# The state-mixing layer of a four-layer encoder step, with its low-rank branches first and its key and decay work spread over the projections

## The reference

```
xx = h_prev - h;  xm[i] = h + xx * mu[i]          # six mixes: xr xw xk xv xa xg
r = xr @ w_rkv[0];  k = xk @ w_rkv[1];  v = xv @ w_rkv[2]
w_log = -softplus(-(w0 + tanh(xw @ w1) @ w2)) - 0.5;  decay = exp(-exp(w_log))
a = sigmoid(a0 + (xa @ a1) @ a2);  g = sigmoid(xg @ g1) @ g2
kk = k * k_k, divided by its norm over each head
k = k * (1 + (a - 1) * k_a)
S = S * decay + (S @ -kk) (kk * a)^T + v k^T;  y = S @ r   # per token
y = groupnorm(y) * ln_w + ln_b + sum(r * k * r_k) * v;  out = (y * g) @ w_out
```

## Time and profile before

| what | value |
|---|---|
| median of three runs | 1920.26 us |
| the profiled execution's own time | 1920.77 us |
| its span in the trace | 1918.8 us |
| PE busy | 1689.6 us, 88% of the span |
| weight load (PEld) busy | 1604.2 us, 84% |
| DVE busy | 1190.7 us, 62% |
| ACT busy | 841.1 us, 44% |
| POOL busy | 739.6 us, 39% |
| mean granted clock of TensorE | 0.941 |

### The profile page before, as it was taken

One profiled execution on the slowest core, in us unless ns is written; L12 is line 12 of the kernel. 1 busy time (PEld: TensorE's weight loads), 2 busy tenths in 40 slices (PEclk: granted clock), 3 DMA queues, 4 the chain that ended last, 5 costly groups with the idle time before them and its releaser, 6 DMA issues.

```text
span 1918.8 us, 37370 instructions
## 1 busy us (share of the span) xinstructions
PE 1689.6 (88%) x14101; PEld 1604.2 (84%) x14101; DVE 1190.7 (62%) x2041; ACT 841.1 (44%) x1561; POOL 739.6 (39%) x829
## 2 busy tenths in 40 slices
PE   4988999996776299799999968799999987999995
PEld 3867999995763299799999957699999975999994
DVE  3685777645526845567774446667774586677832
ACT  2444566432225033345653334456553345466532
POOL 5651566300011541036651116346641670366501
PEclk9998999997888599899999989899999988999997
DMA  6312555452320000345545511145544620455451
GB/s 154 115 46 86 141 146 152 136 154 85 110 66 6 0 3 10 95 124 145 149 135 149 157 41 49 57 132 153 153 130 141 169 83 23 135 150 153 127 150 59
DMA packets 342621, 204.95 MB, mean 107 GB/s; under 512 B 20898, under 2 KB 339640, under 8 KB 342384
## 3 DMA queue, kind: packets, MB, share of 16 engines
q1 hardware_dynamic: 338704, 196.27, 35.8%
q0 software_dynamic: 3808, 7.17, 1.4%
HBM read 199.92 MB, written 3.39 MB: 106 GB/s over the span
## 4 chain that ended last, share of the span: by engine, by line
PE 79%; DVE 10%; ACT 4%; POOL 3%; issue 3%; DMA 1%; ACTq 0%; DVEq 0%; POOLq 0%
PE bank L873 22%; PE bank L874 22%; PE bank L875 22%; PE bank L1149 4%; PE bank L884 2%; ACT LS L1471 1%; PE bank L1109 1%; DVE XX L2083 1%; ACT hi L1437 1%; DVE SW L1995 1%; DVE LS L1863 1%; DVE LS L1854 1%; DVE SC L1981 1%; POOL vrows L621 1%; DVE top L1992 1%
## 5 line engine op out<-in xcount | busy, mean ns | idle before, releaser
L873 PE MATMUL bank<-XH,hi 128*128 128x320 f32 (+2 forms) x2024 | 637.0, 315 | 32.9 <-issue 12.2
L1809 DVE TENSOR_TENSOR lo<-raw,hi 128x2048 fp32r<-128x2048 f32 (+4 forms) x201 | 425.7, 2118 | 360.6 <-ACT hi L1437 360.6
L874 PE MATMUL bank<-XL,hi 128*128 128x320 f32 (+2 forms) x2024 | 632.4, 312 | 0.0
L875 PE MATMUL bank<-XH,lo 128*128 128x320 f32 (+2 forms) x2024 | 632.1, 312 | 0.0
L873 PEld LDWEIGHTS bank<-XH,hi 128*128 128x128 f32 (+1 forms) x2024 | 382.9, 189 | 39.7 <-issue 26.4
L1437 ACT ACTIVATE hi<-raw 128x2048 fp32r<-128x2048 f32 (+3 forms) x205 | 359.6, 1755 | 72.4 <-PE bank L875 64.2
L874 PEld LDWEIGHTS bank<-XL,hi 128*128 128x128 f32 (+1 forms) x2024 | 383.2, 189 | 1.1
L875 PEld LDWEIGHTS bank<-XH,lo 128*128 128x128 f32 (+1 forms) x2024 | 382.8, 189 | 0.5
L685 POOL TENSOR_TENSOR upad<-upad,rstd 128x128 f32<-128x128 f32 (+1 forms) x176 | 168.6, 977 | 199.6 <-ACT upad L1517 199.6
L873 PE MATMUL bank<-GH,hi 128*128 128x322 f32 x704 | 219.2, 311 | 0.0
L874 PE MATMUL bank<-GL,hi 128*128 128x322 f32 x704 | 218.8, 311 | 0.0
(11 more groups left out here) (378 smaller groups left out, 2427.4 us busy)
## 6 DMA issues: line engine op xcount, KB each, us to landing
raw<-in_f_w_up SPq DMA_DIRECT2D x176, 512.0 KB, 5.0
raw<-in_f_w_down SPq DMA_DIRECT2D x64, 704.0 KB, 4.7
raw<-in_a_w_in SPq DMA_DIRECT2D x12, 1024.0 KB, 5.2
raw<-in_b_w_rkv SPq DMA_DIRECT2D x12, 1024.0 KB, 5.2
raw<-in_a_w_out SPq DMA_DIRECT2D x8, 1024.0 KB, 5.1
raw<-in_b_w_out SPq DMA_DIRECT2D x4, 1024.0 KB, 5.6
raw<-in_c_w_out SPq DMA_DIRECT2D x4, 1024.0 KB, 5.2
raw<-in_a_w_in SPq DMA_DIRECT2D x12, 256.0 KB, 4.2
```

What stands on the lines that cost most here:

```text
L873: pe.matmul(out, a, xh(k), start=(start and k == 0), stop=False)
L874: pe.matmul(out, a, xl(k), start=False, stop=False)
L875: last = pe.matmul(out, b, xh(k), start=False, stop=(stop and k == kt - 1))
L1809: dve.tensor_tensor(lo[n % 2][:, 0:w_], raw[n % 2][:, 0:w_], hi[n % 2][:, 0:w_].bitcast(F32), ALU.subtract).then_inc(w_lo, 1)
```

## The change

Only layer 1's mixer is touched. The order of the products becomes key, receptance, value. The low-rank weights move to where VV and G lie, and POOL loads them as soon as the layer before has made its last output tile; the three low-rank mixes are made first, into LW, A and K. Their first matmuls stand ahead of all products; the second ones go in groups of three between the first four products. The three large mixes are made tile by tile: DVE mixes into one of two small buffers (xn), ACT takes the high part, DVE the low part; the second mix has its own pair XH2, XL2. Products use two banks, not four. Decay, key norms and bonus are spread in the orders of all engines over products 12 to 23, tile by tile with two buffers each. Two exponentials replace three. POOL multiplies the keys, rates and receptance by the decays and the keys by their gain (four instructions a tile), and ACT scales the gate G behind the first chunk's evacuations. The cores of the edits:

```diff
# POOL
-                pool.wait_ge(mm_done, done_after[s0 + 11])
+                pool.wait_ge(x_done, 8 * xs_of[norm_of[layer, "mix"]] + 8)
...
+                for m in range(KD):
+                    pool.wait_ge(kk_used, m + 1)
+                    pool.tensor_tensor(A[:, m, :], A[:, m, :], XX[:, m, :], ALU.mult)
+                    pool.wait_ge(gain_done, m + 1)
+                    chain(pool.tensor_tensor(K[:, m, :], K[:, m, :], TK[:, m % 2, :], ALU.mult))
+                    pool.tensor_tensor(K[:, m, :], K[:, m, :], XX[:, m, :], ALU.mult)
+                    pool.wait_ge(rkv_evac, KD + m + 1)
+                    pool.tensor_tensor(R[:, m, :], R[:, m, :], HN[:, m, :], ALU.mult).then_inc(keys_done, 1)
...
+                pool.wait_ge(keys_done, KD)
+                pool.wait_ge(mm_done, done_after[s0 + 11])
                 side_by_side(0)
# PE
+                pe.wait_ge(lora_in, 96)
...
+                    for k in range(KD):
+                        pe.wait_ge(lora_mix, KD * a + k + 1)
+                        last = pe.matmul(psum[4 + a][r_, 0:T], L1[:, k, c_], (LW, A, K)[a][:, k, :], start=(k == 0), stop=(k == KD - 1))
...
+                def lora_rows(m):
+                    if m == 0:
+                        pe.wait_ge(shift_out, 1)
+                        pe.wait_ge(lora_act, 3)
+                    if m >= 2:
+                        pe.wait_ge(lora_evac, 3 * m - 3)
...
+                def key_sums(m):
+                    if m == 0:
+                        pe.wait_ge(lora_evac, 24)
+                    if m >= 2:
+                        pe.wait_ge(hs_root, m - 1)
+                    pe.wait_ge(kk_sq, m + 1)
+                    pe.matmul(psum[2 + m % 2][:, 0:T], C("headsum"), sq[:, m % 2, :], start=True, stop=True).then_inc(hs_done, 1)
+                def bonus_sums(m):
+                    if m >= 2:
+                        pe.wait_ge(bonus_out, m - 1)
+                    pe.wait_ge(bonus_in, m + 1)
...
+                sums_at = {13: (0, 1), 14: (2, 3), 15: (4, 5), 16: (6, 7)}
+                bonus_at = {19: (0,), 20: (1,), 21: (2, 3), 22: (4, 5), 23: (6, 7)}
+                for i in range(24):
+                    n, j = s0 + i // 2, i // 8
+                    ready(n)
+                    if i >= 2:
+                        pe.wait_ge(rkv_evac, i - 1)
+                    product(psum[i % 2][:, 0:T], n, 128 * (i % 2), lambda k: xh[:, k, :], lambda k: xl[:, k, :],
+                            before=(lambda k: pe.wait_ge(mix_done, KD * j + k + 1)) if i % 8 == 0 else None)
+                    if i < 4:
+                        lora_rows(2 * i)
+                        lora_rows(2 * i + 1)
# ACT
+                def high(j, k):
+                    act.wait_ge(mix_raw, KD * j + k + 1)
+                    act.copy((XH, XH2, XH)[j][:, k, :], xn[:, k % 2, :]).then_inc(mix_hi, 1)
+                def key_squares(m):
+                    if m >= 2:
+                        act.wait_ge(hs_done, m - 1)
+                    act.activation(sq[:, m % 2, :], K[:, m, :], ACT.Square, scale=vcol("b_k_k", m)).then_inc(kk_sq, 1)
+                def key_roots(m):
+                    act.wait_ge(hs_done, m + 1)
+                    if m >= 2:
+                        act.wait_ge(kk_used, m - 1)
+                    act.activation(xn[:, m % 2, :], psum[2 + m % 2][:, 0:T], ACT.Sqrt).then_inc(hs_root, 1)
+                def key_gain(m):
+                    if m >= 2:
+                        act.wait_ge(keys_done, m - 1)
+                    act.activation(TK[:, m % 2, :], A[:, m, :], ACT.Identity, scale=vcol("b_k_a", m), bias=onemka[:, m:m + 1]).then_inc(gain_done, 1)
+                middle(0)
+                high(0, 0)
+                middle(1)
+                highs(0, 1, 8)
+                middle(2)
+                for i in range(4):
+                    tile(i)
+                    if i % 2:
+                        split_hi(s0 + i // 2 + 2)
+                    lora_rows(2 * i)
+                    lora_rows(2 * i + 1)
+                highs(1, 0, 4)
+                tile(4)
+                highs(1, 4, 8)
+                tile(5)
+                split_hi(s0 + 4)
...
+                act.wait_ge(cc_done, KD)
+                chain(act.activation(XX[:, :, :], HN[:, :, :], ACT.Exp, scale=-DECAY))
+                act.activation(HN[:, :, :], HN[:, :, :], ACT.Exp, scale=DECAY).then_inc(decay_done, 1)
+                tile(12)
+                key_gain(0)
+                key_gain(1)
+                tile(13)
+                split_hi(s0 + 8)
+                for i in range(14, 18):
+                    m = 2 * (i - 14)
+                    key_roots(m)
+                    key_roots(m + 1)
+                    if m + 3 < KD:
+                        key_squares(m + 2)
+                        key_squares(m + 3)
+                    tile(i)
+                    if i % 2:
+                        split_hi(s0 + i // 2 + 2)
+                    if m + 3 < KD:
+                        key_gain(m + 2)
+                        key_gain(m + 3)
...
                 turned_parts(0)
+                act.wait_ge(bonus_out, KD)
+                for m in range(KD):
+                    ins = act.activation(G[:, m, :], G[:, m, :], ACT.Copy, scale=vcol("b_ln_w", m))
# DVE
+                mix(0, 0, 8)
+                split_lo(s0 + 1)
+                split_lo(s0 + 2)
+                dve.wait_ge(lora_out, 24)
+                mix(1, 0, 4)
+                split_lo(s0 + 3)
+                mix(1, 4, 8)
+                split_lo(s0 + 4)
+                dve.wait_ge(mm_done, done_after[s0 + 3])
+                mix(2, 0, 4)
+                split_lo(s0 + 5)
+                mix(2, 4, 8)
+                split_lo(s0 + 6)
...
+                def key_heads(m):
+                    dve.wait_ge(hs_root, m + 1)
+                    t = xn[:, m % 2, :]
+                    chain(dve.tensor_scalar(t, t, 1e-12, None, ALU.max))
+                    chain(dve.reciprocal(t, t))
+                    chain(dve.scalar_tensor_tensor(out=t, in0=K[:, m, :], scalar=vcol("b_k_k", m), in1=t, op0=ALU.mult, op1=ALU.mult))
+                    dve.scalar_tensor_tensor(out=chunks(MX[:, m, :], 1, 64), in0=chunks(t, 1, 64), scalar=-1.0,
+                                             in1=chunks(HN[:, m, :], 0, 63), op0=ALU.mult, op1=ALU.mult)
+                    dve.tensor_scalar(chunks(MX[:, m, :], 0, 1), chunks(t, 0, 1), -1.0, None, ALU.mult)
+                    dve.wait_ge(gain_done, m + 1)
+                    dve.tensor_tensor(A[:, m, :], t, A[:, m, :], ALU.mult).then_inc(kk_used, 1)
...
+                key_heads(0)
+                key_heads(1)
+                split_lo(s0 + 8)
+                key_heads(2)
+                key_heads(3)
+                split_lo(s0 + 9)
+                for m in range(4, 8):
+                    key_heads(m)
+                split_lo(s0 + 10)
+                dve.wait_ge(kk_used, KD)
+                bonus_rows(0)
+                bonus_rows(1)
+                split_lo(s0 + 11)
+                for m in range(KD):
+                    bonus(m)
+                    if m + 2 < KD:
+                        bonus_rows(m + 2)
```

More of the change, by code:

```diff
@@ L361, in build @@
         VV = take("VV", [128, KD, T])
-        LW = take("LW", [128, KD, T])
+        over_s = over + 7 * size([128, KD, T])
+        take = region(over_s + size([128, KD, T]))
         G = take("G", [128, KD, T])
@@ L1112, in pe_rwkv @@
[L1112 to L1116, removed]
-                                  start=True, stop=True).then_inc(lora_out, 1)
[L1119 to L1124, removed]
@@ L1664, in evac @@
+                for i in range(18, 24):
+                    tile(i)
+                    if i == 19:
+                        split_hi(s0 + 11)
                 def evac(name, c, dst):
@@ new lines, in mixed, with mix, low @@
+                def mixed(dst, k, mu):
+                    return dve.scalar_tensor_tensor(out=dst, in0=XX[:, k, :], scalar=vcol("b_mu", 8 * mu + k),
+                                                    in1=HN[:, k, :], op0=ALU.mult, op1=ALU.add)
+                for a, mu in enumerate((1, 4, 5)):
+                    for k in range(KD):
+                        mixed((LW, A, K)[a][:, k, :], k, mu).then_inc(lora_mix, 1)
+                def mix(j, first, end):
+                    lows = (XL, XL2, XL)[j]
+                    def low(k):
+                        dve.wait_ge(mix_hi, KD * j + k + 1)
+                        dve.tensor_tensor(lows[:, k, :], xn[:, k % 2, :], (XH, XH2, XH)[j][:, k, :].bitcast(F32), ALU.subtract
+                                          ).then_inc(mix_done, 1)
+                    for k in range(first, end):
+                        if KD * j + k >= 2:
+                            dve.wait_ge(mix_done, KD * j + k - 1)
+                        mixed(xn[:, k % 2, :], k, (2, 0, 3)[j]).then_inc(mix_raw, 1)
+                        if k > first:
+                            low(k - 1)
```

(13 more changed lines are left out.)

191 lines of the change are left out of this document (70 added, 121 removed).

## The result

The changed kernel takes 1868.26 us in the median of four runs (1866.00 to 1870.22), against 1920.22 (1919.88 to 1923.24) for the kernel before on the same chip: 0.9726 of its time, 95% interval 0.9708 to 0.9743, so 52 us less. The forecast was 1876 us, with 1863 to 1890 as its range.

A forecast was written before the change was run, and what follows sets the result against it. PE, busy 88% of the span, was taken to be shortenable only where it waits in layer 1's mixer. The walk moved the second stage from 678.15 to 633.5, gaining 44.6 us from 1920.77: 1876 us, range 1863 to 1890.

The forecast's parts named there:

- the walk: Prediction's step-by-step sum through layer 1's mixer, from weight loads to the first chunk's second stage at 633.5 us.
- Rival A: Key-head stretch: the round through DVE, POOL and ACT sets the pace, about 13 to 17 us each; 1876 us; chance 0.50.
- One sign: Timeline from about 539 to 595 us: PE should be mostly idle at the low clock.
- Rival D: Layer 1's mixer: products hide everything and PE is the bound; gain of 96 us, 1825 us; chance 0.05.
- E: POOL's 12 path instructions held up by DVE's two-input ones; at 6.4 us each 1942 us; slower, chance 0.03.
- F: No change: time comes back because the recurrence or output slab loads end at a fixed time; chance 0.02.
- Rival B: Key-head rounds without the lock's charges: 8.2 us less, 1864 to 1869 us; chance 0.19.
- the lock's charge: Key-head rounds, DVE and POOL blocking each other: 0.9 us a round, and 2.3 in the first two; 8.2 in sum.
- The step on the rounds: Four pairs of key-head tiles handed round DVE, POOL and ACT: 56.7 us in sum, ending at 595.3.
- the stalls: Products 4 to 11, waiting for evacuations with two banks: five small stalls of 0.8 to 1.1 us, 4.3 in sum.
- the slow restart of 3.0: PE after standing since product 19: 3.0 us extra around products 20 to 23.
- the scalings: Eight scalings of G on ACT ahead of the first square's evacuation: 8 x 0.55 = 4.4 us on the path.

The follow-up runs named there:

- the experiment: Changed kernel with DVE making the ninth slab's low part before the first key_heads, not behind the second: 1863.26 us in one run.
- two load semaphores: Changed kernel with the first low-rank matmuls waiting for the first three weight loads only, the second ones for the other three: 1865.41 us in one run.
- the four edits: Changed kernel with key gains behind the roots, gate scalings on POOL, ninth slab's low part first and two groups of weight loads: 1848.53 us.
- The last edit: Changed kernel with the four edits plus ACT's inverse square root in place of root and DVE reciprocal: 1841.17 us, 0.9595 of the kernel before.

## Why the prediction was right, and where its sum was off

Its steps against the changed kernel's trace, in us after the norm's reciprocal (those of the walk less 433.98):

| point | walk | trace |
|---|---|---|
| first low-rank matmul | 10.6 | 11.0 |
| third nonlinearity done | 30.9 | 30.0 |
| last of the second low-rank matmuls ends | 55.2 | 52.5 |
| product 11 out | 87.7 | 83.4 |
| exponentials done | 98.9 | 94.0 |
| first pair's clip | 104.6 | 99.4 |
| last `key_heads` done | 161.3 | 152.1 |
| bonus sums end | 185.7 | 176.3 |
| second stage of the first chunk | 199.5 | 188.4 |

So this stretch gave 244.2 - 188.4 = 55.8 us, where 44.6 were forecast. Two things took a part back: the 96 matmuls at the lower clock 2.4, and a layer that began 2.9 later in this execution. 55.8 - 2.4 - 2.9 = 50.5, and the profiled times differ by 50.55. So close an agreement is partly luck: what follows those 96 matmuls took from 1235.6 to 1237.6 us in the ten traces. It is luck too that the two took back half of what the walk had overstated: it missed the second stage by 11 us, and the profiled time missed the forecast by only 6 (8 in the median).

**The bound was named rightly.** Rival A, the round through three engines, is what the trace shows, by pair distances, by the key gain's wait for POOL, and by POOL's busy time (33.0 in 56 us, 28 forecast; the difference is stretched instructions). Moving the two key gains of each round gave 11.9 us. One sign held only in part: PE was to be idle mostly and at the low clock, and worked for 27 of 56 us at a granted clock of 0.77, between the two levels. Rival D, PE as the bound, is excluded by PE's 27 busy us of 56; E by POOL's instructions, the longest of which took 2.84 in the rounds and 2.92 behind them; F because the gain of the stretch arrived at the end of the kernel. Rival B is wrong in what it denies, though its time (1864 to 1869) holds the median: the lock's charge is there, one low part costing 2.0 us in the experiment. The time came out at B's end for other reasons.

**The mis-sized terms**, in order. The step on the rounds was too long: 16.5, 16.5, 14.2 and 9.5, together 56.7, measured 15.24, 15.26, 13.37 and 8.86, together 52.7. `key_heads` took 4.0 and, beside POOL, 4.7, not 4.3 and 5.2; the charge for the low part was 2.3 and measured 2.0. The second low-rank matmuls were priced at 3 x 0.57 = 1.71 a group and took 1.475: two of the three run together, though each step is then 0.74 long and not 0.57. That is 1.9 us over eight groups. The first-stage ones took 15.2 instead of 16.5; the records of two branches overlap there too (454.06 starts within the line above it). Of products 4 to 11, the stalls were 4.3 by the walk and 2.7 measured (83.4 - 52.5 = 30.9 us, where eight at 3.52 are 28.2). From product 11 to the first clip it took 16.0 where the walk has 16.9. At the end the slow restart of 3.0 was close (2.5), the scalings cost 3.7, not 4.4, and they began 0.9 earlier, because ACT's evacuations ahead of them ran beside PE's work and not after it. Every one of these errors is under 3 us but the rounds, and nearly all have the same sign; that is why they made 11 us. In `key_heads` the steps of the reciprocal (2.19) and of the product behind it (0.58) came out as priced; the error lies in the clip (0.36, not 0.48) and in the instructions that don't wait for one another, whose records overlap (0.48 for two, not 0.59; 0.40, not 0.47).

**Slips in the prediction's own working**: the third nonlinearity, from 463.5 with 1.28 and 0.43, ends at 465.2, not 464.9. The POOL instruction of 6.39 us is a scaling by a vector, and others of its kind took 1.08, not the 0.86 of the product it is compared with. The range begins at 1863, 1 below B's lower end. None of this moves the forecast by more than 1 us.

**Not seen at all**: that the pause of the scalings would put the stage behind it on the lower clock (2.4 us), and that DVE's mixes follow the loads so closely that the two nearly tie.

**The second buffers** did what the walk says: the gaps of 5.75 are gone, and taking the overlap away from one change of mix cost 6.8. What the other parts of the change gave one by one (the early weight loads, the interleaved low-rank matmuls, the tile-by-tile key work) no run separates.

The Trainium skill (TensorEngine Tiling (Array Packing), section "Overview") holds that a contraction over 64 rows or fewer leaves TensorE underused, and that splitting it into independent tiles can be up to twice as fast there. Here two such matmuls of different branches, whose operands lie in different halves of the partitions, took 0.74 us together, as long as the single one over 128 rows behind them, with nothing set for it in the code. Against twice 0.57 that is about 1.5 times as fast; with the slower third one it bears on this kernel by 1.9 us.

What stays open: the restart took from 20.15 to 21.03 us in the changed kernel and in all its edits but the last. In the changed kernel full-speed records (0.31 us) come back 5.0 us after it begins, with two load semaphores 3.3. The length of the idle time ahead of it does not order these (1.87 us with the four edits, 20.17; 6.17 with two load semaphores, 20.15; 7.69 in the changed kernel, 20.85). What decides this was not tried, and it makes single differences under 1 us of this stretch unsafe to read. The last edit differs plainly: PE was at full-speed records already and stood for only 0.77 us, and the stretch took 18.65.

## What to carry to other kernels

When work is spread over three engines in a ring, look at every queue for an instruction that waits for the previous turn and stands ahead of the next one's first: moving such a pair in each of three turns gave 12 us here without removing any work. Put a long DVE instruction with two SBUF inputs where POOL rests, not beside it. Price a pause of PE by its restart as well, and before speeding up what releases a wait, ask what would release it next and how far behind that is.

## What the runs showed of the hardware that was not expected

- Under short alternating instructions both sides of DVE and POOL lose: 0.86 became 0.94 to 1.20 on POOL and about 0.5 became 1.04 on DVE, and a DVE clip with one SBUF input went from 0.32 to as much as 1.00. The one long instruction cost POOL 2.0 us at a time.
- A pause of PE of 4.26 us made the following 96 small matmuls take 5.39 us instead of 3.02; with a pause of 0.73 they took 3.02. In the traces of other edits with the same pause they took 4.24 to 5.38.
- Weight loads issued from POOL were not slowed: the last wait for them is 7.62 us here and 7.63 before, and POOL took 3.78 for five issues against 3.79.
- ACT's inverse root took the place of the root with no further table load, and saved DVE a reciprocal of 2.15 us a tile.
